# A GeGLU down-projection by seven products: weights' loads, their fifth place, the last three couples and the final norms rearranged

## The reference, cut to what matters

```
h = rms_norm(x, norm_ffn_pre) * (1.0 + sc2) + sh2
u = conv3(h @ w_up) + conv_b            # 512 x 11264
a, b = split(u, 2)                      # 512 x 5632 each
y = (gelu(a) * b) @ w_down              # 512 x 2048, w_down is 5632 x 2048
x = x + g2 * rms_norm(y, norm_ffn_post)
```

## Time and profile before

| | us |
|---|---|
| median of 3 runs | 2429.55 (2429.44 to 2430.79) |
| profiled execution, own time | 2431.21 |
| profiled execution, span | 2429.4 |
| TensorE busy | 2313.9 (95%) |
| VectorE busy | 1887.9 (78%) |
| ScalarE busy | 1103.1 (45%) |
| first matmul of the down-projection, from the span's start | 1958.96 |
| last matmul ends | 2407.24 |
| last output made by VectorE | 2426.71 |

### The profile page before, as it was taken

How to read it: one execution, slowest core, us unless ns; L and a number is a source line. 1 busy time by engine, 2 the same in 40 slices (tenths; PEclk the granted TensorE clock), 3 DMA queues, 4 the chain that set the end, 5 groups by cost and what they waited for, 6 DMA issues and landing times.

```text
span 2429.4 us, 36942 instructions
## 1 busy us (share of the span) xinstructions
PE 2313.9 (95%) x13613; PEld 2032.6 (84%) x13613; DVE 1887.9 (78%) x2416; ACT 1103.1 (45%) x1495; POOL 111.3 (5%) x185
## 2 busy tenths in 40 slices
PE   2899999999999999989999999999999989999996
PEld 2777778888888878868999999999999967788875
DVE  6965667787777763267899999999999967889888
ACT  5356743333333342264444444444444434554553
POOL 1010000000000000000000000000000000000000
PEclk9899999999999999989999999999999999999998
DMA  9952456676666525235655555555555477655564
GB/s 371 336 143 71 143 174 215 200 240 210 209 206 215 190 70 183 95 121 144 174 143 145 143 143 143 144 142 143 142 142 143 108 241 255 231 182 198 186 255 156
DMA packets 371311, 430.90 MB, mean 177 GB/s; under 512 B 14268, under 2 KB 291012, under 8 KB 368928
## 3 DMA queue, kind: packets, MB, share of 16 engines
q1 hardware_dynamic: 354704, 369.74, 47.8%
q0 software_dynamic: 16528, 60.15, 10.2%
HBM read 407.27 MB, written 54.54 MB: 190 GB/s over the span
## 4 chain that ended last, share of the span: by engine, by line
PE 82%; DVE 7%; DMA 6%; ACT 2%; issue 2%; SPq 1%; DVEq 0%; ACTq 0%
PE bank L1973 24%; PE bank L1974 24%; PE bank L1975 24%; DMA DRAW<-in_w_down_dram 3%; PE bank L2130 2%; DVE W_lo L1842 2%; DMA W_raw<-t_dram 2%; DMA ADA<-in_w_ada_dram 1%; PE bank L2039 1%; PE bank L2162 1%; DVE ACC L1305 1%; DVE GS_lo L1839 1%; PE bank L2149 1%; DVE DRAW L1820 1%; PE bank L2030 1%
## 5 line engine op out<-in xcount | busy, mean ns | idle before, releaser
L1973 PE MATMUL bank<-H_lo,W_hi 128*128 128x256 f32 (+1 forms) x1888 | 660.3, 350 | 3.3 <-DVE H_lo L1320 3.3
L1975 PE MATMUL bank<-H_hi,W_lo 128*128 128x256 f32 (+1 forms) x1888 | 635.8, 337 | 0.0
L1974 PE MATMUL bank<-H_hi,W_hi 128*128 128x256 f32 (+1 forms) x1888 | 635.6, 337 | 0.0
L1973 PEld LDWEIGHTS bank<-H_lo,W_hi 128*128 128x128 f32 x1888 | 360.3, 191 | 42.7 <-issue 7.7
L1974 PEld LDWEIGHTS bank<-H_hi,W_hi 128*128 128x128 f32 x1888 | 360.3, 191 | 39.5 <-issue 7.7
L1975 PEld LDWEIGHTS bank<-H_hi,W_lo 128*128 128x128 f32 x1888 | 359.6, 190 | 37.9
L1973 PE MATMUL bank<-T_lo,W_hi 128*128 128x256 f32 x1280 | 362.2, 283 | 0.0
L1974 PE MATMUL bank<-MGR,W_hi 128*128 128x256 f32 x1280 | 362.2, 283 | 0.0
L1975 PE MATMUL bank<-MGR,W_lo 128*128 128x256 f32 x1280 | 362.2, 283 | 0.0
L1973 PE MATMUL bank<-W_lo,GS_hi 128*128 128x512 f32 x616 | 243.6, 395 | 20.1 <-DVE W_lo L1842 20.0
L1259 DVE TENSOR_TENSOR W_lo<-W_raw,W_hi 128x1024 fp32r<-128x1024 f32 x138 | 168.3, 1220 | 104.7 <-ACT W_hi L709 104.3
(11 more groups left out here) (279 smaller groups left out, 3618.9 us busy)
## 6 DMA issues: line engine op xcount, KB each, us to landing
AB_raw<-in_w_ada_dram SPq DMA_DIRECT2D x128, 512.0 KB, 4.5
UB<-in_w_up_dram SPq DMA_DIRECT2D x100, 512.0 KB, 4.1
W_raw<-in_w_in_dram SPq DMA_DIRECT2D x90, 512.0 KB, 4.7
t_dram<-in_w_down_dram POOLq DMA_DIRECT2D x66, 512.0 KB, 7.6
W_raw<-in_w_up_dram SPq DMA_DIRECT2D x56, 512.0 KB, 4.0
W_raw<-in_w_down_dram SPq DMA_DIRECT2D x56, 512.0 KB, 4.2
DRAW<-in_w_down_dram SPq DMA_DIRECT2D x54, 512.0 KB, 4.1
ADA<-in_w_ada_dram SPq DMA_DIRECT2D x32, 512.0 KB, 5.7
```

What stands on the lines that cost most here:

```text
L1973: pe.matmul(acc, st_hi, mv_lo, start=start, stop=False)
L1974: pe.matmul(acc, st_hi, mv_hi, start=False, stop=False)
L1975: return pe.matmul(acc, st_lo, mv_hi, start=False, stop=stop)
```

## The change

Five things are changed; nothing is computed otherwise.

1. `load_g` uses four semaphores, and its wait is for the couple two earlier: `gs_hi` of (0, m - 2, 0), none for m below 2.
2. The raw weights get a fifth place, `DRAW4`; unit d goes to place d % 5. The load of d waits for the split of unit d - 5, and, where that unit's raw block is still wanted for a sum, for that sum (`sum_ready`); unit 4 waits only for the end of the up-projection.
3. The last three couples go product by product: 19, 20, 21 of product 2, then of product 4. TensorE then runs couple 19's product 2 whole, 20 and 21 of product 2 for tile 0, then for tile 1, couple 19's product 4 whole, and 20 and 21 of product 4 by tile.
4. VectorE adds and gates tile 0 ahead of the last unit's split; each tile's norm (`finish`) stands behind the next tile's sums and gate. ScalarE takes tile t's root after tile t + 1's squares, and the last two roots together.
5. On GpSimd `GROW2` is loaded after sweep 0, and the four tiles of `X1` at units 118, 126, 134 and 142.

```diff
-DOWN[-3], DOWN[-2] = DOWN[-2], DOWN[-3]
+DOWN[-6:] = sorted(DOWN[-6:], key=lambda unit: (unit[2], unit[1]))
+
+DOWN_RAW = 5
...
-            W_raw[:, 0, :], W_raw[:, 1, :]]
+            W_raw[:, 0, :], W_raw[:, 1, :], at("DRAW4", [P, 1024], F32, 60 * KB)[:, :]]
...
-                sp.dma_start(g_pair(m), g_dram[2 * m:2 * m + 2].rearrange("t p n -> p t n")).then_inc(g_landed[m % 2], 16)
+                sp.dma_start(g_pair(m), g_dram[2 * m:2 * m + 2].rearrange("t p n -> p t n")).then_inc(g_landed[m % 4], 16)
...
-                elif d < SLOTS:
+                elif d < 4:
                     sp.wait_ge(lo_ready, U_DOWN - 1)
-                else:
-                    sp.wait_ge(lo_ready, U_DOWN + partner(d - SLOTS) + 1)
+                elif d < DOWN_RAW:
+                    sp.wait_ge(unit_used, U_DOWN)
+                else:
+                    before = d - DOWN_RAW
+                    sp.wait_ge(lo_ready, U_DOWN + before + 1)
+                    if partner(before) > before:
+                        sp.wait_ge(sum_ready, 2 * (FT - PLAIN) + W_SUMS[partner(before) + 1])
...
-                    sp.wait_ge(gs_hi, DOWN.index((0, m, 0)) + 1)
+                    if m >= 2:
+                        sp.wait_ge(gs_hi, DOWN.index((0, m - 2, 0)) + 1)
                     load_g(m + 2)
...
-            pool.wait_ge(unit_used, U_DOWN)
+            pool.wait_ge(unit_used, U_DOWN + SWEEP_AT[1])
             pool.dma_start(GROW2[:, :], gate_dram[1:2, :].partition_broadcast(P)).then_inc(grow_landed, 16)
 
-            pool.wait_ge(gs_lo, SWEEP_AT[3] + KT)
             pool.wait_ge(x1_stored, 16 * TT)
             for tt in range(TT):
+
+                pool.wait_ge(gs_lo, SWEEP_AT[3] + 8 * tt + 8)
                 pool.dma_start(X1[:, tt, :], x1_dram[tt * P:(tt + 1) * P, :]).then_inc(x1_landed, 16)
...
-            for tt in range(TT):
-                last_squares(tt)
-                act.wait_ge(y_summed, tt + 1)
-                act.activation(col(SM, RSY + tt), col(SM, RSY + tt), ACT.Sqrt, bias=col(SM, EPSC), scale=1.0 / D)\
-                    .then_inc(y_rms, 1)
+            for b in range(8):
+                last_square(b)
+                if b in (3, 5):
+                    y_root(b // 2 - 1)
+            y_root(TT - 2)
+            y_root(TT - 1)
...
+                if d == len(DOWN) - 1:
+                    last_sums(0, (0, 1))
+                    gate_y(0, (0, 1))
                 down_low(d)
...
+            for tt in range(1, TT - 1):
+                last_sums(tt, (2 * tt, 2 * tt + 1))
+                gate_y(tt, (2 * tt, 2 * tt + 1))
+                finish(tt - 1)
+            last_sums(TT - 1, (6,))
+            gate_y(TT - 1, (6,))
+            last_sums(TT - 1, (7,))
+            finish(TT - 2)
+            finish(TT - 1, (7,))
...
+            last_banks((d0 + 3, d0 + 4), 0, (0, 1)).then_inc(y_tile_done, 1)
+            last_banks((d0 + 3, d0 + 4), 1, (0, 1), True).then_inc(y_tile_done, 1)
+            down_unit(d0 + 5, (d0 + 5) % 4, 4, False, False)
+            last_banks((d0 + 6, d0 + 7), 2, (0, 1)).then_inc(y_tile_done, 1)
+            last_banks((d0 + 6, d0 + 7), 3, (0,)).then_inc(y_tile_done, 1)
+            last_banks((d0 + 6, d0 + 7), 3, (1,)).then_inc(unit_used, 1)
```

More of the change, by code:

```diff
@@ L338, in hybrid_encoder_layer @@
         sum_ready, n1_kept, posted = sem("sum_ready"), sem("n1_kept"), sem("posted")
-        g_stored, g_landed = [sem(f"g_stored{e}") for e in range(2)], [sem(f"g_landed{k}") for k in range(2)]
-        t2_landed, down_landed = sem("t2_landed"), [sem(f"down_landed{k}") for k in range(2)]
+        g_stored = [sem(f"g_stored{e}") for e in range(2)]
+        t2_landed = sem("t2_landed")
+        assert KT == 2 * ADA1_SLOTS
+        g_landed, down_landed, ada1_count = ada1_landed[0:4], ada1_landed[4:7], 2 * 16
         gs_hi, gs_lo, yg_ready, y_squared, y_rms, y_done = (
@@ L1915, in _, with finish @@
                         last_step(n)
-            for tt in range(TT):
-                banks = (6,) if tt == TT - 1 else (2 * tt, 2 * tt + 1)
-                last_sums(tt, banks)
-                gate_y(tt, banks)
-                if tt == TT - 1:
-                    last_sums(tt, (7,))
+            def finish(tt, banks=()):
                 dve.wait_ge(y_squared, 8 + 2 * (tt + 1))
                 dve.tensor_reduce(col(SM, RSY + tt), SM[:, SSY + 4 * tt:SSY + 4 * tt + 4], AX.X, ALU.add).then_inc(y_summed, 1)
-                if tt == TT - 1:
-                    gate_y(tt, (7,))
+                gate_y(tt, banks)
                 dve.wait_ge(y_rms, tt + 1)
@@ L2419, in _, with last_banks @@
                         down_unit(d, d % 4, 4 if d % 2 else 0, False, d >= SWEEP_AT[3] - 2)
-            d0 = len(DOWN) - 4
-            for tt in range(TT - 1):
-                for d in (d0 + 2 * (tt // 2), d0 + 2 * (tt // 2) + 1):
-                    down_ready(d)
-                    for b in (2 * (tt % 2), 2 * (tt % 2) + 1):
-                        ins = down_bank(d % 4, b, b + 4 * (tt // 2), False, d % 2 == 1)
-                ins.then_inc(y_tile_done, 1)
-            for d in (d0 + 2, d0 + 3):
-                ins = down_bank(d % 4, 2, 6, False, d % 2 == 1)
-            ins.then_inc(y_tile_done, 1)
-            for d in (d0 + 2, d0 + 3):
-                down_bank(d % 4, 3, 7, False, d % 2 == 1).then_inc(unit_used, 1)
+            d0 = len(DOWN) - 8
+            for d in range(d0, d0 + 3):
+                down_unit(d, d % 4, 4 if DOWN[d][2] else 0, False, False)
+            def last_banks(units, tt, bs, told=False):
+                for d in units:
+                    down_ready(d)
+                    for b in bs:
+                        ins = down_bank(d % 4, 2 * (tt % 2) + b, 2 * tt + b, False, d == units[-1])
+                    if told and d == units[0]:
+                        ins.then_inc(unit_used, 1)
+                return ins
+            last_banks((d0 + 3, d0 + 4), 0, (0, 1)).then_inc(y_tile_done, 1)
[4 more added lines that the diff above has]
+            last_banks((d0 + 6, d0 + 7), 3, (1,)).then_inc(unit_used, 1)
 _INS = ['x', 'c', 'w_ada', 'b_ada', 'norm_mix_pre', 'norm_mix_post', 'w_in', 'q_norm', 'k_norm',
```

40 lines of the change are left out of this document (22 added, 18 removed).

## The result

| | before | changed |
|---|---|---|
| median, us | 2430.17 (4 runs) | 2401.99 (4 runs, 2401.63 to 2403.0) |
| profiled execution, span | 2429.4 | 2399.8 |
| first matmul of the down-projection | 1958.96 | 1958.12 |
| lost by TensorE inside it | 29.2 | 2.5 |
| last matmul's end E | 2407.24 | 2379.73 |

The ratio of the times is 0.9882, with a 95% interval of 0.9865 to 0.9899: 28.2 us faster, against 28.9 forecast, and 2402.0 against 2400.7.

A forecast was written before the change was run, and what follows sets the result against it. TensorE was taken as the bound, with 29.2 us lost waiting for late weights and an end behind it; gains 24.1 + 2.1 + 2.7 = 28.9 us gave a median of 2400.7 us, range 2397 to 2411.

The forecast's parts named there:

- TensorE's loss inside the stage: Down-projection: 29.2 us lost to late weights and clock restarts; 3.0 of sweep 0's 27.1 stay, gaining 24.1.
- The start: First units of the down-projection: VectorE's own work limits until 1969.2; unit 4's pause shrinks from 6.2 to 0.1 us.
- Rival C: Start of the down-projection: the new order leaves its pauses as they are, 2415.5 us; chance 4%.
- What holds the loads: SyncE's queue in sweep 0: the gated tiles' wait on GS_hi, 79.2 us, holds the loads; raw places the rest.
- The loop of 3.0 + L against 10.88: Sweep 0: VectorE's 3.0 us plus landing time L per two couples, 10.4 us, stays under TensorE's 10.88.
- Bandwidth: Sweep 0: a couple's three 512 KB transfers need 289 GB/s, a share 0.87 of 333 GB/s.
- rival A: Sweep 0: saturated transfers come slower and bind, 2407 to 2410 us; chance 22%.
- GROW2: Its megabyte shared unit 9's 11.5 us landing at the start; loading it in sweep 1 costs nothing.
- X1: Sweep 3: loading its four megabytes one at a time removes a 1.82 us pause, gaining 2.1 us.
- Rival B: Calm sweeps: moved GROW2 and X1 transfers each make a new pause, 43.5 us in all, 2444 us; chance 2%.
- The end: Behind TensorE's last matmul: reordered units and norms put the last output at 16.8 us, not 19.5, gaining 2.7.
- The root's table load: ScalarE at the end: load takes 1.28 us without drain; the skill's 1.38 us drain would cut gain 1.4 at most.

The follow-up runs named there:

- g's part with g in front: Kernel before with only part 1, but each couple of g sent directly ahead of a couple of weights: 2431.01 us; 464.8 us from TensorE's third unit to span end.
- g's part alone: Kernel before with only part 1 (four semaphores for g, wait for the couple two earlier): 2421.57 us; 450.5 us from TensorE's third unit to span end.
- coarse waits: Changed kernel, five raw places kept, but both loads of a couple wait for the partner's split as before: 2411.64 us.
- g's wait back: Changed kernel with g's wait on GS_hi put back to the same couple, all else kept: 2414.03 us.
- old end: Changed kernel with parts 3 and 4 undone, the end as in the kernel before: 2406.57 us.

## Why the prediction was right, step by step

- **TensorE's loss inside the stage** (29.2 us, 3.0 + 0 to be left): 2.5 us are left. The two pauses at the start stayed, 0.46 and 1.19 us, together the forecast 2.2 with their restarts; unit 4 was 0.12 us late for 0.1; the 0.7 us of new small pauses did not come. Shown by the trace after. (The six small pauses that the working counts between 2019 and 2069 us are five; their sum, 5.6 us, is right.)
- **The start**: unit 5's sum at 1968.28, 10.2 us behind the stage's first matmul, the 1969.2 of the working less the 0.8 us by which the stage began earlier. VectorE's own work was the limit there, as said, but for 1.1 us in which it waited for ScalarE's halves of two splits. Rival C falls.
- **What holds the loads**: here a step failed. "SyncE's waits say what holds the loads: 79.2 us on GS_hi" took the length of a wait for its cost. The wait held nothing that the raw places would have let go (g's part with g in front: 464.8 against 464.4); what it cost came by g's place ahead of the weights. The sum was right all the same, since its loop had the landing time as a term, and I had said that it would shorten when the transfers no longer start together: 7.0 to 5.2 us by g's part alone, 8.5 us of the gain by the medians and 13.9 by the tail number.
- **The loop of 3.0 + L against 10.88** held: no steady loop pauses in the changed kernel, nor with coarse waits, where VectorE's term is 1.5 us longer. The landing of 5.6 us left it far from its limit of 7.9, so no run tried it there. With g's wait back it did not, since the loop then has another term, GS_hi, that the formula leaves out.
- **Bandwidth**: 250 / 0.75 = 333 GB/s at full share was the estimate; 329 GB/s at a share of 0.96 was measured (343 at full share). The transfers reached that share at the start and TensorE did not pause for them, so rival A's mechanism did not come. A full share is no fixed rate, though: from 1980 to 1990 us this trace moved 373 GB/s. The Trainium skill ("DMA: Bandwidth & Descriptors", Specifications) gives about 358 GB/s as HBM's limit for a core; with one core at work the measurement lies above it, and the measurement decides. Nothing here went by the difference.
- **GROW2**: rightly a part, 1.5 us by its own run in the changed kernel. It was not the main cause of the 8.7 us before unit 8, since g's part alone, with GROW2 as early as before, brought them to 4.7; its share in them was not tried by itself.
- **X1** (2.1 us for spreading it): mis-attributed. The pause went, but spread or not makes 0.1 us. With four raw places and coarse waits the four megabytes at once still cost a pause of 1.46 us (g's part alone); in the changed kernel they cost none. So the 2.1 us came with part 2 and not with part 5, and which half of part 2 brings them was not tried. Rival B falls: the changed kernel has no pause behind 1972 us, so neither GROW2 nor any of the four X1 makes one.
- **The end** (2.7 us): 2.1 by the run with the old end, 2.2 by the distance behind E, which is 17.2 us where the working had 16.8. VectorE came to tile 0 at E - 10.1, not E - 10.9: its sums, splits and the last of its gating steps stood back to back there, which the working left out. Most of a tile's wait for ScalarE came back, as said (2.48 and 1.05 us).
- **The root's table load** ran in 1.28 us with the root 0.02 us behind it here too, without the drain of 1.38 us that the Trainium skill ("ScalarE: Activation LUTs", What ACT_TABLE_LOAD costs) adds; the measurement decides for this kernel.
- **The sum** (28.9 us): 26.7 gained inside the stage for 26.2 forecast, 2.2 behind it for 2.7. That the total agrees to 0.1 us is luck: two misses of half a microsecond cancel, and X1's 2.1 us came from another part than the one they were booked under. The profiled execution's own time came out at 2401.6 us for 2402.3. The working then took off 1.7 us, by which that execution stood above the median before; the changed kernel's stands 0.4 us *under* its median, and so the median is 1.3 us above the forecast.

Still open: why g's part alone gains 8.5 us by one measure and 13.9 by the other, how g's wait with five places splits into the loads that it holds and the queue that it puts in front, and why the part ahead of the stage moves by 5 us from one execution to another, and later with the coarse waits than with any other edit.

## What to carry to other kernels

A long wait in a queue's table says where the queue stood, not what it cost: ask what the next instruction would have waited for anyway, and what the wait puts directly in front of the transfer that the loop needs. Send what has time to spare behind what has none, give each transfer a wait of its own, and check that a new order of units doesn't hold a buffer longer. In a chain over tiles that two engines share, take each engine's answer for tile t before it starts on tile t + 1's question: that alone gave 4 to 5 us more here.

## What the runs showed of the hardware that I had not expected

- Two 512 KB transfers landed in a median of 6.7 to 7.1 us where a third on the same queue was issued 0.4 to 1.1 us ahead of them, and in 5.2 us where it was issued 0.9 us behind them; the third itself then took 6.7 to 7.0 us in place of 4.4 to 5.3.
- GpSimd needed 3.85 us for a multiply of 128 x 1024 float32 by a column and 3.25 us for an addition while VectorE was at work, and 2.84 and 2.34 us once VectorE had ended (2390.25); VectorE's own outputs stayed at 1.28 us for 1024 columns. Whether it is SBUF that they share was not tried by itself.
- In the kernel before TensorE's granted clock was 0.50, which is 1.2 GHz, behind the pauses of 4.16, 6.06 and 2.35 us, and it did not fall behind those of up to 1.82 us. In the other runs it fell behind 2.87, 3.08, 4.14, 4.26 and 5.29 us, and not behind 2.19.
